# First attention: the weighing of the values in three passes of rounded parts, two items behind, with the rests on GpSimd

## The reference, cut to what matters

```python
s = jnp.einsum('bsgrd,bcgd->bgrsc', q, kc) * ATTN_SCALE
p = masked_softmax(s, mask)
o = jnp.einsum('bgrsc,bcgd->bsgrd', p, v)
...
o_nsa = g[..., 0:1] * o_cmp + g[..., 1:2] * o_sel + g[..., 2:3] * o_win
o_nsa = o_nsa * jax.nn.silu(z_n)
```

## Time and profile before

| | |
|---|---|
| Median of 3 runs | 2997.67 us (2997.52, 2997.67, 3006.53) |
| The profiled execution's own time | 3006.93 us |
| Its span | 3005.2 us |
| TensorE busy in the span | 2915.5 us (97%) |
| The stage `attend_first` | 243.88 to 413.68 us, 169.8 us long |
| DVE, ACT, POOL busy in the stage | 124.3, 86.4, 62.0 us |
| Mean granted TensorE clock in the stage | 0.94 of full |

### The profile page before, as it was taken

One profiled execution on the slowest core, in us unless ns is written; L12 is line 12 of the kernel. 1 busy time (PEld: TensorE's weight loads), 2 busy tenths in 40 slices (PEclk: granted clock), 3 DMA queues, 4 the chain that ended last, 5 costly groups with the idle time before them and its releaser, 6 DMA issues. The chain is left out here.

```text
span 3005.2 us, 43684 instructions
## 1 busy us (share of the span) xinstructions
PE 2915.5 (97%) x16768; PEld 2579.0 (86%) x16768; DVE 2330.6 (78%) x4062; ACT 1122.7 (37%) x1850; POOL 136.8 (5%) x99
## 2 busy tenths in 40 slices
PE   8999989999999999999999999999999999999998
PEld 7885568999999887788999998899999877779997
DVE  5776767799988766567998888798888855578886
ACT  4434545233333423244323234432333423254443
POOL 2431410000000000000000000000000000000000
PEclk9999999999999999999999999999999999999999
DMA  6432042333333250222333333233333230223332
GB/s 190 130 96 71 22 149 74 107 127 108 118 113 107 76 152 22 69 71 85 100 118 119 113 106 92 78 105 120 120 112 106 71 110 14 57 85 99 99 99 92
DMA packets 317538, 292.78 MB, mean 97 GB/s; under 512 B 12562, under 2 KB 269844, under 8 KB 315796
## 3 DMA queue, kind: packets, MB, share of 16 engines
q1 hardware_dynamic: 317332, 289.98, 31.4%
HBM read 284.18 MB, written 2.10 MB: 95 GB/s over the span
## 5 line engine op out<-in xcount | busy, mean ns | idle before, releaser
L2554 PE MATMUL PS<-hid_f,w_hi 128*128 128x512 f32 (+1 forms) x2464 | 563.4, 344 | 6.2 <-DVE hid_f L2770 6.2
L2554 PEld LDWEIGHTS PS<-hid_f,w_hi 128*128 128x128 f32 x2464 | 389.2, 188 | 64.9 <-DVE hid_f L2770 7.6
L2543 PE MATMUL PS<-x_hi_f,w_hi 128*128 128x384 f32 (+1 forms) x1216 | 390.8, 321 | 0.0
L2543 PE MATMUL PS<-x_lo_f,w_hi 128*128 128x384 f32 (+1 forms) x1216 | 390.7, 321 | 0.0
L2543 PE MATMUL PS<-x_hi_f,w_lo 128*128 128x384 f32 (+1 forms) x1216 | 390.6, 321 | 0.0
L2554 PE MATMUL PS<-hid_f,w_lo 128*128 128x512 f32 x1232 | 338.8, 344 | 0.0
L2635 ACT ACTIVATE w_hi<-w_raw 128x512 fp32r<-128x512 f32 (+1 forms) x420 | 244.4, 603 | 202.7 <-DMA w_raw<-in_w_ffn_dram 142.2
L2135 DVE SCALAR_TENSOR_TENSOR ada_product<-ada_w,ada_s 128x1024 f32<-128x1024 f32 x228 | 278.4, 1221 | 28.0 <-DMA ada_w<-in_w_ada_dram 24.1
L2543 PE MATMUL PS<-t_hi_f,w_hi 128*128 128x384 f32 (+1 forms) x912 | 293.3, 322 | 0.0
L2543 PE MATMUL PS<-t_lo_f,w_hi 128*128 128x384 f32 (+1 forms) x912 | 293.0, 321 | 0.0
L2543 PE MATMUL PS<-t_hi_f,w_lo 128*128 128x384 f32 (+1 forms) x912 | 293.0, 321 | 0.0
(11 more groups left out here) (394 smaller groups left out, 5315.8 us busy)
## 6 DMA issues: line engine op xcount, KB each, us to landing
w_raw<-in_w_ffn_dram SPq DMA_DIRECT2D x256, 512.0 KB, 4.6
ada_w<-in_w_ada_dram SPq DMA_DIRECT2D x120, 512.0 KB, 3.5
w_raw<-in_w_in_dram SPq DMA_DIRECT2D x46, 512.0 KB, 6.0
w_raw<-in_w_out_dram SPq DMA_DIRECT2D x24, 512.0 KB, 7.0
ada_s<-in_conditions_dram SPq DMA_DIRECT2D x7, 1024.0 KB, 5.2
ada_room<-in_w_ada_dram SPq DMA_DIRECT2D x14, 512.0 KB, 3.2
q_plain<-in_w_ada_dram SPq DMA_DIRECT2D x10, 512.0 KB, 5.4
w_raw<-in_w_ffn_dram SPq DMA_DIRECT2D x16, 256.0 KB, 2.8
```

The lines of the kernel that those rows point to most:

```text
L2543: last = nc.tensor.matmul(bank_of(kind), wt[:, k, :], xt[:, k0 + k, :], start=(k == 0 and one == 0), stop=(k == 3 and one == 2))
L2554: last = nc.tensor.matmul(ps[:, a:e], wt[:, f, :], hid[:, f, v, a:e], start=(start and f == 0 and one == 0), stop=(end and f == n - 1 and ...
```

## The change

1. The values are split once, ahead of the first item: ACT rounds them (`V_hi`, `Vc_hi`, two instructions), POOL subtracts (`V_lo`, `Vc_lo`, two instructions).
2. For each item ACT, after the exponential, rounds it (`E_hi`), and POOL subtracts the rounded part, over the same memory (`E_lo` lies where `E` lay). `E_hi` and `E_lo` have three buffers.
3. `weigh(n)` is three products of rounded (fp32r) operands in place of one float32 product, and waits for POOL's rest. It now stands behind `score(n + 2)`.
4. `keep(i - 1, 1)` moves from the first to the second item of unit `i` in ACT's queue. On POOL each item's rest comes in its place among `spread_max` and `add`, and `add(i - 2)` stands where `add(i - 1)` stood.
5. `tmp` lies in the memory of `T`. Some semaphores are shared with other stages.

```diff
             def weigh(n):
-                pe.wait_ge(expd, n + 1)
+                pe.wait_ge(e_rest, n + 1)
+                if n == 0:
+                    pe.wait_ge(v_rest, 2)
...
-                nc.tensor.matmul(c.PS[0:66, 4 + g, :], v, e, start=(kt == 0), stop=(kt == u.tiles - 1)).then_inc(weighed, 1)
+                e_hi, e_lo = E_hi[rows_of, n % NE, :], E_lo[rows_of, n % NE, :]
+                for one, (v, e) in enumerate(((v_hi, e_hi), (v_lo, e_hi), (v_hi, e_lo))):
+                    last = nc.tensor.matmul(c.PS[0:66, 4 + g, :], v, e, start=(kt == 0 and one == 0), stop=(kt == u.tiles - 1 and one == 2))
+                last.then_inc(weighed, 1)
...
                 score(n)
-                if n >= 1:
-                    weigh(n - 1)
+                if n >= 2:
+                    weigh(n - 2)
...
                 nc.scalar.activation(E[0:k, n % NE, :], c.PS[0:k, 2 + n % 2, :], ACT.Exp, scale=SCALE).then_inc(expd, 1)
+                act.wait_ge(expd, n + 1)
+                nc.scalar.activation(E_hi[0:k, n % NE, :], E[0:k, n % NE, :], ACT.Copy).then_inc(e_rounded, 1)
...
             move(0)
+            nc.scalar.activation(V_hi[:], Vx[:], ACT.Copy).then_inc(v_rounded, 1)
+            nc.scalar.activation(Vc_hi[:], Vc[:], ACT.Copy).then_inc(v_rounded, 1)
             for n, (i, g, kt) in enumerate(items):
                 exp(n)
-                if n == first[i] and i >= 1:
+                if n == first[i] + 1 and i >= 1:
                     keep(i - 1, 1)
                 if n == last_item(i, 0) + 1:
                     keep(i, 0)
...
+            def rest(n):
+                k = CMP_PAD if units[items[n][0]].branch == "cmp" else P
+                pool.wait_ge(e_rounded, n + 1)
+                if n > 0:
+                    pool.wait_ge(e_rest, n)
+                nc.gpsimd.tensor_tensor(E_lo[0:k, n % NE, :], E[0:k, n % NE, :], E_hi[0:k, n % NE, :].bitcast(F32), ALU.subtract).then_inc(e_rest, 1)
+                pool.wait_ge(e_rest, n + 1)
...
             for i in range(n_units):
-                if i + 2 < n_units:
-                    spread_max(i + 2)
-                if i >= 1:
-                    add(i - 1)
+                for n in range(first[i], first[i + 1]):
+                    rest(n)
+                    if n == first[i]:
+                        if i + 2 < n_units:
+                            spread_max(i + 2)
+                    if n == first[i] + 1 and i >= 2:
+                        add(i - 2)
+            add(n_units - 2)
             add(n_units - 1)
```

More of the change, by code:

```diff
@@ L1300, in _ @@
                                                 valid[:], None, ALU.mult))
+    for t in norm_steps:
+        t.n += 1
 class FirstUnit:
@@ L1316, in __init__, with attend_first @@
         self.row_items = HEADS // self.per_row
-def attend_first(c, sb, rows, O, Q, KK, KL, KKc, KLc, Vx, Vc, topk, negeye, rounded, gates, dram, share):
+def attend_first(c, sb, rows, O, Q, KK, KL, KKc, KLc, Vx, Vc, T, topk, negeye, rounded, gates, dram, share):
     nc = c.nc
@@ L1339, in attend_first @@
     Mx = sb("row_max", [P, 3, GROUPS, 68])
-    E = sb("exp_t", [P, 3, 512])
+    NE = 3
+    with scope(nc) as plain:
+        E = plain("exp_t", [P, NE, 512])
+    E_lo, E_hi = sb("exp_lo", [P, NE, 512], F32R), sb("exp_hi", [P, NE, 512], F32R)
+    V_hi, Vc_hi = sb("v_hi", [P, QT, 6, 66], F32R), sb("vc_hi", [CMP_PAD, GROUPS, 66], F32R)
+    (Vx, V_lo), (Vc, Vc_lo) = Vx, Vc
     OT = sb("o_turned", [66, GROUPS, 512])
@@ L1343, in attend_first @@
     chosen_mask = sb("chosen", [P, 9 * P], F32R)
-    co, tmp = sb("co", [P, 2, HEADS]), sb("o_tmp", [P, 2, HEADS, HD])
+    co, tmp = sb("co", [P, 2, HEADS]), T.rearrange("p i (h d) -> p i h d", h=HEADS)
     first, row_first = [0], [0]
@@ L1476, in _ @@
                     back(i - 1)
+            weigh(len(items) - 2)
             weigh(len(items) - 1)
@@ L1650, in _ @@
             finish(n_units - 1)
+    for t in of_items:
+        t.n += len(items)
 class Unit:
@@ L2167, in first_block @@
         rows = sb1("first_rows", [P, QT, ROW_COLS])
-        Vx = sb1("first_v", [P, QT, 6, 66])
+        with scope(nc) as plain:
+            Vx = plain("first_v", [P, QT, 6, 66])
+        V_lo = sb1("first_v_lo", [P, QT, 6, 66], F32R)
         T = sb1("cmp_t", [P, 2, SEQ])
@@ L2187, in first_block @@
             KKc, KLc = sb2("KKc", [P, GROUPS, CMP_PAD], F32R), sb2("KLc", [P, GROUPS, CMP_PAD], F32R)
-            Vc = sb2("Vc", [CMP_PAD, GROUPS, 66])
+            with scope(nc) as plain:
+                Vc = plain("Vc", [CMP_PAD, GROUPS, 66])
+            Vc_lo = sb2("vc_lo", [CMP_PAD, GROUPS, 66], F32R)
             s_c, room = sb2("ada_s", [P, 2, D]), sb2("ada_room", [P, 3, D])
@@ L2197, in first_block @@
             with scope(nc) as sb:
-                attend_first(c, sb, rows, O, Q, KK, KL, KKc, KLc, Vx, Vc, topk, tabs[0], rounded, gates, dram, rest)
+                attend_first(c, sb, rows, O, Q, KK, KL, KKc, KLc, (Vx, V_lo), (Vc, Vc_lo), T, topk, tabs[0], rounded, gates, dram, rest)
 class Refill:
```

30 lines of the change are left out of this document (20 added, 10 removed).

## The result

| | before | after |
|---|---|---|
| Median (4 runs each) | 2999.19 us | 3047.36 us |
| Lowest to highest | 2997.52 to 3006.53 | 3042.88 to 3050.37 |
| The profiled execution and its span | 3006.93, 3005.2 | 3050.37, 3048.6 |
| The stage | 243.88 to 413.68, 169.8 us | 242.73 to 463.10, 220.4 us |

The changed kernel is slower: ratio 1.0156, 95% interval 1.0143 to 1.0168, some 47 us where the forecast had 31.7. The measured 3047 lies inside the stated range, 3002 to 3054, and above the forecast's own, 3018 to 3041. In the two profiled executions the stage is 50.6 us longer; what lies ahead of it and behind it took 7.2 us less (1.1 and 6.0), which leaves the 43.4 us by which the spans differ.

What follows compares the result with a forecast made beforehand. TensorE, busy 97% of the span, was taken as the bound. Terms 3.2 + 0 + 10.5 + 0 + 16.0 + 2.0 = 31.7 us raised the median from 2997.67 to 3029 us; range 3002 to 3054, the forecast's own 3018 to 3041.

Steps and rivals of the forecast that it cites:

- Start: Stage start: the first keep waits for a weighing behind the second unit's first score, POOL's rest runs late; +3.2 us.
- Dense units 1, 2, 4, 5: 28 items: TensorE's saving of 4.8 us offset by waits of 1.2 us for each of four units; sum 0.
- Units 3, 6 to 10: Units of two items: ACT's chain of 7.5 us sets the pace; +1.75 us for each of six, +10.5.
- Units 11, 12: ACT and POOL need 16 to 19 us where the units take 22.06; 0.
- Units 13 to 15 and the end: POOL's work and DVE's products one after the other, +16.0 us; rounding and rest before the last keep, +2.0.
- low end of 1.10: POOL's rest per item: taken as 1.36 us, with 1.10 kept as the low end.
- The exclusion: POOL's instructions and DVE's modulation products go one after the other, whole; 14.9 us of products in units 13 to 15.
- POOL would be busy over 85% from unit 11 on: Sign in the changed kernel's trace: POOL busy over 85% from unit 11 on, TensorE waiting for its rests there.
- the clock rival: Units 6 to 15: a waiting TensorE is granted less clock, say 0.85; priced at 12 us, 3041 us; chance 0.17.
- TensorE's saving shows: Whole stage: TensorE stays the bound, -11.6 + 2.0 = -9.6 us, 2988 us; chance 0.10.
- POOL is hidden, ACT isn't: Last units: DVE's products find gaps in POOL's queue, the 16 us fall away; +10.9, 3009 us; chance 0.18.
- Nothing moves: Whole stage: the chain offsets the three passes, any sum within 9 us; "same" was given 0.16.

Runs made afterwards that it cites:

- run 1: Changed kernel without POOL's 68 rests; the third product reads the rounded exponential again: 3030.2 us.
- run 2: Changed kernel with DVE's 22 modulation products on 8 of 1024 columns: 3037.6 us.
- run 10: Changed kernel with the turning back one score later and the modulation products on 8 of 1024 columns: 3024.6 us.
- run 4: Changed kernel with the turning back one score later on TensorE: 3034.7 us.
- run 3: Changed kernel with POOL's spread behind the rest of the unit's second item, not its first: 3045.8 us.
- run 6: Changed kernel with the turning back one score later and keep(i, 0) one item later on ACT: 3035.1 us.
- run 5: Old kernel with the new order alone (weighing two items behind, second keep one item later), no rounding or rests: 3014.6 us.
- run 11: Changed kernel with later turning back and keep, without rests and without ACT's separate rounding: 3004.1 us.
- run 12: Changed kernel in the old order (weighing one item behind), three passes, without rests or separate rounding: 2999.8 us.
- run 8: Changed kernel with later turning back and keep, without POOL's rests: 3009.6 us.
- run 7: Changed kernel with sixteen idle TensorE products of 120 columns ahead of each turning back: 3062.0 us.

## Why the prediction came out as it did

The direction was right, and the start, the short units and the last ones cost about what the forecast gave them. Two places that the sum put at nothing, the dense units and units 11 and 12, cost 19 us in the profiled executions; in the median the forecast was some 15 us short. Forecast and measured, by the prediction's places (from first exponentials, as above):

| | forecast | measured |
|---|---|---|
| Start | +3.2 | +2.4 |
| Dense units 1, 2, 4, 5 | 0 | +12.7 |
| Units 3, 6 to 10 | +10.5 | +11.1 |
| Units 11, 12 | 0 | +6.3 |
| Units 13 to 15 and the end | +18.0 | +18.0 |
| Sum | 31.7 | 50.5 |

**Prices.** The instructions that the rests and the products became, over the stage (busy us, mean ns):

```profile
L1558 POOL TENSOR_TENSOR exp_lo<-exp_t,exp_hi 128x512 fp32r<-128x512 f32 x60 | 86.1, 1435 | 35.1 <-ACT exp_hi L1526 29.6 <-POOL exp_lo L1558 3.4 <-PE PS L1442 1.2
L2176 DVE SCALAR_TENSOR_TENSOR ada_room<-ada_room,ada_s 128x1024 f32<-128x1024 f32 x22 | 42.3, 1923 | 0.8
```

A rest alone takes 1.25 to 1.30 us, near the 1.27 of the rows and not the low end of 1.10. From one rest to the next that waits for it pass 1.45 us (442.38 to 443.84), where the prediction took 1.36. The parts of the values cost nothing, as forecast: behind them POOL still waited 0.48 us for ACT's maxima, at 255.83.

**The exclusion** is, instruction by instruction, as the prediction had it. POOL's timeline in units 12 and 14:

```profile
396.73 1.29 POOL L1558 TENSOR_TENSOR exp_lo<-exp_t,exp_hi 128x512 fp32r<-128x512 f32 x1 [0.17 <-POOL exp_lo L1558]
398.10 3.88 POOL L1572 TENSOR_TENSOR qr<-row_max_t,neg_eye 4x512 fp32r<-4x512 f32 x2
...
424.82 2.05 POOL L1558 TENSOR_TENSOR exp_lo<-exp_t,exp_hi 128x512 fp32r<-128x512 f32 x1 [0.17 <-ACT exp_hi L1526]
427.04 2.05 POOL L1558 TENSOR_TENSOR exp_lo<-exp_t,exp_hi 128x512 fp32r<-128x512 f32 x1 [0.17 <-POOL exp_lo L1558]
```

and DVE's in the same moments:

```profile
396.77 2.34 DVE L2176 SCALAR_TENSOR_TENSOR ada_room<-ada_room,ada_s 128x1024 f32<-128x1024 f32 x1
...
399.14 1.94 DVE L2176 SCALAR_TENSOR_TENSOR ada_room<-ada_room,ada_s 128x1024 f32<-128x1024 f32 x1
...
401.01 1.28 DVE L1628 TENSOR_REDUCE row_max<-PS 128x1 f32<-128x512 f32 x2
...
423.64 2.10 DVE L2176 SCALAR_TENSOR_TENSOR ada_room<-ada_room,ada_s 128x1024 f32<-128x1024 f32 x1
...
425.78 2.17 DVE L2176 SCALAR_TENSOR_TENSOR ada_room<-ada_room,ada_s 128x1024 f32<-128x1024 f32 x1
```

In unit 14 rest and product go by turns, 2.05 and 2.10 us where each takes 1.27 and 1.22 alone. The Trainium skill ("SBUF — State Buffer", section "SBUF: two separate sides") calls this an exclusive lock; the rows agree. It takes both sides: without rests (run 1) the products harm units 11-12 no more than without products (run 2) the rests do, 22.0 and 21.7 us for the old 22.1. With the turning back moved out of the way it is worth 4.3 us in unit 12 and 10.3 in units 13-15 (run 10 against run 4), 14.6 in all; in the changed kernel itself 4.0 us in unit 12 and 7.8 in units 13-15 (run 2). The forecast had 14.9, but all of it in units 13-15, where the items would have been held anyway, at 41.1 us without the products (run 2) and at 38.1 without rests (run 1): there the term was too large, and the group's sum of 18.0 came out right by luck, because a second limit, at the units' heads, lay close behind. The prediction's sign that POOL would be busy over 85% from unit 11 on held in units 13-15 (44.1 of 48.9 us) and not in 11-12 (17.9 of 28.4).

**"Units 11 and 12: 0" failed**, by 3.5 us in unit 11 and 2.8 in unit 12. For unit 12 the working added up ACT's and POOL's busy time and left out DVE's queue. A product began with a rest, and took 2.34 us; the spread behind it took 3.88 us where two of its instructions take 2.03; the second product took 1.94. Behind both products, at 401.01, DVE reads the maxima for which TensorE waits:

```profile
398.87 0.40 PE L1460 MATMUL PS<-exp_lo,v_hi 128*66 128x512 f32 x1
401.75 0.50 PE L1394 MATMUL PS<-KK,Q 128*128 128x512 f32 x1 [2.48 <-DVE row_max L1628]
```

2.48 us of idle time, and half clock behind it. The products were 1.84 us longer than two alone (2 x 1.22), most of that wait. What cost time here was not POOL's delay but that of the reduction behind DVE's products.

Unit 11 has no product. TensorE's turning back there and unit 11 as a whole, in the changed kernel and in run 2:

```profile
386.61 1.14 PE L1470 MATMUL PS<-ident,o_turned 66*128 66x66 f32 x8 [1.70 <-ACT o_turned L1532]
381.98:395.06 13.08, 11.38 (x45) 8.24 (x45) 5.95 (x13) 7.29 (x14) 8.88 (x8) 0.74 0.00 0
...
384.59 0.72 PE L1470 MATMUL PS<-ident,o_turned 66*128 66x66 f32 x8 [1.70 <-ACT o_turned L1532]
379.96:390.31 10.35, 8.65 (x45) 6.18 (x45) 6.21 (x13) 7.30 (x14) 8.88 (x8) 1.00 0.00 0
```

The wait is the same 1.70 us, and the other engines are as busy. In the changed kernel what follows runs at half clock, granted 0.74 over the unit, in run 2 at full clock, and the unit is 2.7 us shorter. So most of unit 11's loss is the clock alone; why it fell in one of the two is not shown.

**"Dense units: sum 0" failed**, by 6.0 and 3.0 us in units 1 and 2, 1.0 and 2.7 in units 4 and 5, and not by the wait that it priced. TensorE's timeline at the head of unit 2:

```profile
290.59 0.40 PE L1460 MATMUL PS<-exp_lo,v_hi 128*66 128x512 f32 x1
...
293.28 0.81 PE L1470 MATMUL PS<-ident,o_turned 66*128 66x66 f32 x8 [2.06 <-ACT o_turned L1532]
293.85 0.78 PE L1439 MATMUL PS<-Q,KK 128*128 128x512 f32 x1
294.42 0.63 PE L1442 MATMUL PS<-qr,KL 68*128 68x512 f32 x1
294.85 0.63 PE L1460 MATMUL PS<-exp_hi,v_hi 128*66 128x512 f32 x1
...
296.55 0.73 PE L1439 MATMUL PS<-Q,KK 128*128 128x512 f32 x1
```

The turning back waits 2.06 us here, 1.25 on average (17.5 us in 14 waits); the forecast had 1.2. But what follows runs at half clock, 0.43 us a product, and the next item takes 296.55 - 293.85 = 2.70 us where one takes 1.45. That is the clock rival, some 1.2 us at this head, in the very units for which the prediction left it out; the Trainium skill ("TensorE: Matmul & The Clock Gate", section "What's actually happening") has the throttled state as the default that activity releases, and the rows agree in so far as half clock follows this wait, while in run 2 full clock stayed through one of 1.70 us. Unit 1 has a second cause, which the start's term had too small. POOL:

```profile
267.55 2.03 POOL L1572 TENSOR_TENSOR qr<-row_max_t,neg_eye 4x512 fp32r<-4x512 f32 x2 [8.34 <-ACT row_max_t L1515]
269.66 1.25 POOL L1558 TENSOR_TENSOR exp_lo<-exp_t,exp_hi 32x512 fp32r<-32x512 f32 x1
```

and TensorE:

```profile
270.96 0.69 PE L1460 MATMUL PS<-exp_hi,vc_hi 32*66 32x512 f32 x1 [4.93 <-POOL exp_lo L1558]
```

A rest stood behind the spread of unit 2, which waited 8.34 us for ACT's moved maxima; TensorE waited 4.93 us for it. It was at half clock already before this wait, from 263.0, and stayed there until 279.8. Run 1 gives 7.1 of the 9.0 us of units 1-2 back, run 3, which puts the spread behind that rest, 3.5. In units 4 and 5, where the rests change nothing (run 1), the later turning back does (run 4: 3.1 us in units 3-5, 2.4 of them in unit 5).

**The short units were right in size and, in the main, by the mechanism named.** ACT's two keeps in units 6 and 7:

```profile
347.83 0.57 ACT L1532 ACTIVATE o_turned<-PS 66x512 f32<-66x512 f32 x1
350.79 0.59 ACT L1532 ACTIVATE o_turned<-PS 66x512 f32<-66x512 f32 x1 [2.40 <-PE PS L1460]
...
355.28 0.57 ACT L1532 ACTIVATE o_turned<-PS 66x512 f32<-66x512 f32 x1
359.75 0.59 ACT L1532 ACTIVATE o_turned<-PS 66x512 f32<-66x512 f32 x1 [3.90 <-PE PS L1460]
```

Between them lie 2.40 us of idle time and a `keep`, the forecast's 2.1 with hand-overs, and unit 6 takes 7.45 us for the forecast's 7.5; at half clock, in unit 7, the idle time is 3.90. Taking the rests away wins nothing (run 1), as it should by a chain in which POOL has no part; moving the turning back and a keep gives 2.1 and 3.5 us back with rounding and rests in place (runs 4 and 6). But not all of the chain counted: the old kernel with the new order alone, without the rounding, already loses 5.3 us there (run 5), and with the turning back and the keep moved the rounding is worth nothing (run 11). A part of the 11.1 us is the clock, as in unit 7, which took 8.97 us.

**Two slips in the working** change little. Units 6 to 15 would take some 108 us by the sum's own terms, not the 114 with which the falling clock was priced; and the low end of the forecast's own range comes out nearer to 3020 than to 3018.

**Rivals.** *TensorE's saving shows* fell: even run 12 has it in units 13-15 only. *POOL is hidden, ACT isn't* fell by runs 2 and 10. *The clock falls* came true beside the forecast, not in its place, and earlier in the stage than it was priced: it is a part of the missing 15 us. How large a part is not shown; in unit 11 it is 2.7 us. *Nothing moves* fell.

**What stays open.** In runs 8, 11 and 12 units 6-10 were granted 0.84, 0.85 and 0.94 where the old kernel had 1.00, with TensorE busy about 90% of the group; why the clock is lower there was not found; run 7 raised it there, in the changed kernel, only from 0.91 to 0.92. So the stage's loss is traced to the rests, the order and the rounding, but how much of each is waiting and how much is half clock stays open.

## What to carry to other kernels

A product split into rounded passes must be charged with who makes the parts: here 0.17 us per item were saved on TensorE for 0.62 on ACT and 1.3 to 1.45 on POOL. To put a consumer one item later moves a wait to every place where something stands right behind it in the queue; move that as well (run 4 gave back 12.7 us by moving two lines). Where POOL works beside DVE, look at which queue stands behind the instruction that loses the turn, and not only at the sum of the busy times.

## What was not expected of the hardware

A rest on 32 partitions takes what one on 128 takes (1.25 and 1.26 us, at 269.66 and 271.07). The exclusion holds for small instructions too, on either side: the spread, on 4 partitions, took 3.88 us beside two products, and in run 2 a product of 8 columns, 0.17 us elsewhere, took 1.27 us (at 392.02) beside a rest. And the granted clock of the start, whose work is nearly the same in all kernels, was anything from 0.62 (run 12) to 0.90 (before).
